# Composing the Fourier channel transform with the mixing weight, in a two-layer fp32 kernel with two more layers behind it

## The chip, the cores and the metric

One core of one Trainium2 chip. The metric is the device time of one execution in microseconds; a version's time is the median of its runs. The core's engines are TensorE (PE), ScalarE (ACT), VectorE (DVE), GpSimd (POOL) and SyncE (SP); SP and POOL issue the DMAs here.

## The reference

Four layers in sequence on 256 tokens of 2048 features; the change touches layers 0 and 1. There the input projection gives, among others, `u_f` of 1024 features in 8 groups of 128. What matters:

```
ug = u.reshape(B, S, 8, 128).astype(float32)
f  = real(fftn(ug, axes=(1, 3), norm="ortho"))   # over the tokens and over a group's channels
y  = einsum("bsgc,gcd->bsgd", f, w_fmix)         # a 128x128 matrix per group
y_f = y * silu(z_f)
```

The Fourier transform over the channels is a fixed 128x128 matrix (a cosine part and a sine part), and so is a map on the same index as `w_fmix[l][g]`. The rest of a layer is low-rank attention, gates, an output projection, a modulation from `c` (shift, scale, gate by the 2048 x 6144 matrix `w_ada[l]`) and two LayerNorms.

## The kernel before

**Plan and engines.** A Python class `Plan` (its method `whole`, L1096) writes one list of steps; then each engine's program (`sync` L1384, `gpsimd`, `tensor`, `scalar`, `vector`) walks that list and emits its own part of every step, in the list's order. So an engine's order is the plan's order, and an instruction that waits holds back what stands behind it on its engine.

**Weights.** Work comes as jobs, one per weight tile of two 128-row blocks (512 KB at most). `prep` (L163) issues the load into a slot on SP's queue (18 slots while the first stage lasts, 9 after it) and, for products in two halves, the split: ACT copies the tile to `whi` (the hi part, L1893 under the step `split`), DVE subtracts it to `wlo` (the lo part, L2214). PE then makes hi x hi, hi x lo and lo x hi products into the banks PM. `run` (L181) emits a job's products some jobs after its load and split; while the plan is `starting`, three jobs behind whatever their kind, later three weight tiles behind.

**Side work.** Everything small (rope, latent norms, Fourier groups, attention heads) is a generator with a `yield` per stage; `round` (L119) advances up to six of them once, twice per weight tile. Their products go to the banks PB: two while the first stage lasts, four later (`banks`).

**The Fourier groups**, `fourier(g)` in `mla` (L627), eight per layer, four started by `u_out` of each half of `u`:

1. `fs_mm` (L1736): two fp32 products with CSS, the transform over tokens, evicted by ACT (`fs`) to a `pbuf`.
2. `fc_mm` (L1743): two fp32 products with CF, cosine on columns 0 to 128 and sine on 129 to 255, evicted by ACT (`fc`) to a `ptbuf`.
3. `fw_mm` (L1750, product L1754): one fp32 product of 256 columns with `w_fmix[g]` in AR at FM; `fw` (L2019, L2431): ACT copies columns 0 to 128 to Z, DVE adds and subtracts the reflected sine part.

**The first stage.** `whole` interleaves the modulation of layer 0 (shift and scale; `ada_pe`, PE products of width 32 on raw tiles, `adap` and `adap_col`) with layer 0's first 24 weight tiles. There are eight k-pairs q; for each q three tiles j0, j1, j2 (one of three column groups each), with modulation tiles between them, and transposes (`trans`) of the normed input for the next q. Hooks `pre` and `after` hang steps on a job. After k-pair 5 the last rope table (`turn`) is made and `begin0` runs `mla_begin`, by which POOL loads `w_fmix` (L1454).

**Later.** Layer 0's gate part of the modulation and layer 1's modulation come as DVE multiply-adds (`ada`, L2127 on AC) between the other tiles. `ada_row` (POOL, L1464) stores a gate row and loads it, spread over the partitions, into GT; the output step of the layer reads GT on DVE (L2377). `w_out` ends a layer; in its fourth tile `late` adds `ln_load` (POOL, L1473), the two LayerNorm vectors of 1024 KB each. At the border `lead` (L1070) writes `post_norm` and `ln`, two normed quarters (`xn`), the sums of the scale's accumulators (`ada_col`, by `columns`), three transposes and the next layer's `begin` (so its `mla_begin`).

Of the kernel before, what the change touches and what calls it, by code (L numbers as in the profile page):

```python
# [61 lines left out]
class Plan:  # L62
# [364 lines left out]
    def post_norm(self, l):  # L427
# [28 lines left out]
        return self.step("post_norm", **s)  # L456

    def gate_post(self, l, blocks):
        def post(pair, mm):
# [69 lines left out]
    def w_out(self, l, w):  # L529
        for g in range(4):  # L530
            def late(g=g):
                if g == 0:
                    self.y_rest()
                    if l < 2:
                        self.ln_in = self.tick("ln_landed", 32)
                        self.step("ln_load", l=l, scores=("score_mm", self.count["score_mm"]))
                    if l == 2:
                        self.toep = self.tick("toep_landed", 96)
                        self.step("toep_windowed", logits=("sm_logit", self.count["sm_logit"]), pool=self.pool_mm)
            self.group([(w, g * 512, 512)], B2, self.out_post(l, g), late=late, early=l, final=g == 3)  # L540
# [3 lines left out]
    def mla(self, l):  # L544
# [3 lines left out]
        def begin():  # L548
            arf.extend(self.ar)
            Tk["fm"] = self.tick("fm_landed", 16)  # L550
            self.step("mla_begin", l=l, free=tuple(arf))

# [74 lines left out]
        def fourier(g):  # L627
# [10 lines left out]
            b, fr = yield from self.take(self.banks)  # L638
            mm = self.tick("fc_mm")
            self.step("fc_mm", bank=b, free=fr, buf=i, fs=a)  # L640
            self.pbuf.put(i, mm)
            yield
            i, ifree = yield from self.take(self.ptbuf)
            a = self.tick("fc")
            self.step("fc", bank=b, buf=i, bfree=ifree, mm=mm)
            self.banks.put(b, a)
            yield
            yield
            b, fr = yield from self.take(self.banks)
            mm = self.tick("fw_mm")  # L650
            self.step("fw_mm", g=g, bank=b, free=fr, buf=i, fc=a, fm=Tk["fm"])
            self.ptbuf.put(i, mm)
            yield
# [415 lines left out]

    def lead(self, first, trans, layer, columns=None):  # L1070

        n = len(self.jobs)
        begin = layer()

        def lead():
            first()
            self.normed((0, 1))
            if columns:
                columns()
            trans((0, 1, 2))  # L1080
            begin()

        def more(q):
            if q < 3:
                self.normed((q + 1,))
            trans((q + 2,))
            if q == 5:
                self.zw = self.h[KT - 1]
        self.jobs[n]["first"] = lead
        for q in range(8):  # L1090
            self.jobs[n + q]["fresh"] = True
        for q in range(1, 6):
            self.jobs[n + q]["pre"] = lambda q=q: more(q)
        return n

    def whole(self):  # L1096
# [27 lines left out]
        self.jobs.extend(ada[0][0])  # L1124

        def cols(q):
            ada[q][1]()
# [16 lines left out]
        for q in range(8):  # L1144
            j0, j1, j2 = (first[8 * g + q] for g in range(3))
            j0["last_chunk"] = q == 7
            self.jobs.append(j0)
            if q == 0:
# [44 lines left out]

        n1 = self.lead(norm1, lambda qs: self.mod_h(1, qs), lambda: self.mla(1), scale)
        self.w_out(1, "w_out1")
# [58 lines left out]
def build(nc, A):  # L1254
    with ExitStack() as ctx:
# [67 lines left out]
        def ar(o, n):  # L1323
            return AR[:, o:o + n]
# [92 lines left out]
        def gpsimd(e):  # L1417
# [30 lines left out]
            for kind, s in plan.order:  # L1448
                if kind == "biases":
# [3 lines left out]
                    e.dma_start(scr[32:64, :], AR[0:32, 2560:2944]).then_inc(SEM["scr_landed"], 16)  # L1453
                elif kind == "mla_begin":  # L1454
                    q.wait_all(s["free"])
                    e.dma_start(ar(FM, 1024).rearrange("p (g d) -> p g d", g=8),
# [43 lines left out]
        def tensor(e):  # L1500
# [7 lines left out]
            for kind, s in plan.order:  # L1508
# [227 lines left out]
                elif kind == "fs_mm":  # L1736
# [5 lines left out]
                    ins.then_inc(SEM["fs_mm"], 1)  # L1742
                elif kind == "fc_mm":  # L1743
                    q.wait_ge(s["fs"])
                    q.wait_all(s["free"])
                    T = pbuf(s["buf"])
                    for t, o in enumerate((slice(0, 129), slice(129, 256))):
                        ins = mm(B[:, o], CF[:, t, :], T[:, o], t == 0, True)
                    ins.then_inc(SEM["fc_mm"], 1)
                elif kind == "fw_mm":  # L1750
                    q.wait_ge(s["fc"])
                    q.wait_ge(s["fm"])
                    q.wait_all(s["free"])
                    e.matmul(B[:, 0:S], ar(FM + s["g"] * 128, 128), ptile(s["buf"])[:, 0:S], start=True, stop=True).then_inc(  # L1754
                        SEM["fw_mm"], 1)
                elif kind == "score_mm":
# [130 lines left out]
        def scalar(e):  # L1887
# [7 lines left out]
            for kind, s in plan.order:  # L1895
# [115 lines left out]
                elif kind == "fs":  # L2011
                    q.wait_ge(s["mm"])
                    q.wait_all(s["bfree"])
                    act(pbuf(s["buf"])[:, 0:S], B[:, 0:S]).then_inc(SEM["fs"], 1)
                elif kind == "fc":
                    q.wait_ge(s["mm"])
                    q.wait_all(s["bfree"])
                    act(ptile(s["buf"])[:, 0:S], B[:, 0:S]).then_inc(SEM["fc"], 1)
                elif kind == "fw":  # L2019
# [695 lines left out]
```

## Time and profile before

| what | value |
|---|---|
| median of 3 runs | 1558.52 us (1557.95 to 1561.76) |
| the profiled execution's own time | 1556.26 us |
| its span | 1554.4 us |
| granted TensorE clock, mean | 0.99 |
| PE busy | 1486.9 us, 96% |
| DVE, ACT, POOL busy | 1065.7, 706.8, 45.3 us |
| DMA | 347.15 MB, mean 223 GB/s |

The span is the time between the first and the last instruction of the profiled execution; the execution's own time has 1.86 us more around it. PE's ends are modelled, so that PE busy is not PE at its peak. An fp32 product is written as two records. The chain of work that ended last is followed back from the last instruction, at each step to what released it; "issue" is time in which the engine waited for nothing that the profile shows.

### The profile page before, as it was taken

The page shows a single profiled execution, that of the slowest core. Times are in us where ns is not written, and L with a number is a line of the kernel's source. Part 1 is how long each engine was busy: PE and PEld are TensorE (multiplying, and loading weights), DVE is VectorE, ACT ScalarE, POOL GpSimd, SP SyncE. Part 2 cuts the span into 40 slices and gives each one's busy share as a digit, 9 for nine tenths or more (in the row PEclk, how much of TensorE's full clock was granted, in tenths as well). Part 3 has the DMA queues.
Part 4 walks back from the last instruction along what each step waited for, and adds up shares of the span by engine and source line. Part 5 has one row for each costly group of instructions (what it writes and reads, how often), then busy time and mean ns, then how long its engine had stood idle before and what let it go on. Part 6 is the DMA issues. An engine that isn't in the chain of part 4 may idle for free.

```text
span 1554.4 us, 25460 instructions
## 1 busy us (share of the span) xinstructions
PE 1486.9 (96%) x10123; PEld 1316.1 (85%) x10123; DVE 1065.7 (69%) x1732; ACT 706.8 (45%) x1218; POOL 45.3 (3%) x66
## 2 busy tenths in 40 slices
PE   5999999989979999999979999999998999999999
PEld 3778789988869788998859997799987998889987
DVE  3348689899987667577575684875655667775653
ACT  2235234344345445444335444654444546665442
POOL 3000000000000000000000000010000000000000
PEclk9999999999989999999999999999999999999999
DMA  9999889998837556776745555466665554445673
GB/s 357 406 406 330 283 294 364 348 365 338 329 90 266 191 195 207 251 247 205 217 148 179 177 169 151 123 219 187 184 196 163 151 162 121 124 123 160 183 223 98
DMA packets 102126, 347.15 MB, mean 223 GB/s; under 512 B 11392, under 2 KB 21876, under 8 KB 101240
## 3 DMA queue, kind: packets, MB, share of 16 engines
q1 hardware_dynamic: 96888, 327.42, 62.7%
q0 software_dynamic: 5120, 18.11, 3.5%
q8 instruction: 80, 1.31, 0.3%
q14 instruction: 38, 0.31, 0.1%
HBM read 343.27 MB, written 2.21 MB: 222 GB/s over the span
## 4 chain that ended last, share of the span: by engine, by line
PE 78%; DVE 11%; issue 4%; DMA 4%; ACT 3%; SPq 0%; DVEq 0%; ACTq 0%
PE PM L1506 66%; PE PB L1506 8%; DVE wlo L2214 2%; DMA stg<-in_w_in 2%; DVE AC L2127 2%; ACT whi L1893 1%; DVE X L2127 1%; DMA stg<-in_w_ada 1%; ACT AR L1893 1%; PE PB L1741 1%; PE PB L1713 1%; PE PB L1816 1%; DVE SM L2127 0%; PE PB L1788 0%; ACT Hh L1893 0%
## 5 line engine op out<-in xcount | busy, mean ns | idle before, releaser
L2214 DVE TENSOR_TENSOR wlo<-stg,whi 128x1024 fp32r<-128x1024 f32 (+2 forms) x417 | 497.9, 1203 | 324.5 <-ACT whi L1893 322.2
L1893 ACT ACTIVATE whi<-stg 128x1024 fp32r<-128x1024 f32 (+2 forms) x417 | 430.3, 1038 | 455.2 <-PE PM L1506 348.5
L1506 PE MATMUL PM<-Hh,whi 128*128 128x256 f32 x1824 | 526.2, 291 | 11.5 <-DVE wlo L2214 7.6
L1506 PE MATMUL PM<-Hh,wlo 128*128 128x256 f32 x1776 | 500.3, 285 | 0.0
L1506 PE MATMUL PM<-Hl,whi 128*128 128x256 f32 x1824 | 497.7, 284 | 0.0
L1506 PEld LDWEIGHTS PM<-Hh,whi 128*128 128x128 f32 x1824 | 352.4, 193 | 29.5 <-issue 17.0
L1506 PEld LDWEIGHTS PM<-Hh,wlo 128*128 128x128 f32 x1776 | 343.6, 193 | 0.0
L1506 PEld LDWEIGHTS PM<-Hl,whi 128*128 128x128 f32 x1824 | 342.5, 193 | 0.4
L1506 PE MATMUL PM<-whi,Hh 128*128 128x512 f32 (+1 forms) x576 | 223.3, 389 | 0.4 <-DVE wlo L2214 0.4
L1506 PE MATMUL PM<-wlo,Hh 128*128 128x512 f32 (+1 forms) x576 | 220.1, 383 | 0.0
L1506 PE MATMUL PM<-whi,Hl 128*128 128x512 f32 (+1 forms) x576 | 218.3, 384 | 0.0
L2127 DVE SCALAR_TENSOR_TENSOR AC<-stg,CA,AC 128x1024 f32<-128x1024 f32 x120 | 153.6, 1280 | 6.6 <-DMA stg<-in_w_ada 4.0
L1506 PEld LDWEIGHTS PM<-whi,Hh 128*128 128x128 f32 x576 | 108.3, 188 | 23.4 <-issue 1.5
L1506 PEld LDWEIGHTS PM<-wlo,Hh 128*128 128x128 f32 x576 | 108.3, 188 | 21.0 <-issue 0.2
L1506 PEld LDWEIGHTS PM<-whi,Hl 128*128 128x128 f32 x576 | 107.1, 188 | 21.4
L1506 PE MATMUL PM<-whi,ARL 128*128 128x512 f32 (+1 forms) x272 | 86.1, 383 | 0.0
L1893 ACT ACTIVATE AR<-PB 128x384 f32<-128x384 f32 (+2 forms) x110 | 47.3, 471 | 75.4 <-PE PB L1506 28.0
L1506 PE MATMUL PB<-AR 64*128 64x256 f32 (+4 forms) x576 | 71.1, 353 | 3.5 <-ACT AR L1893 2.2
L1506 PEld LDWEIGHTS PB<-AR 64*128 64x128 f32 (+2 forms) x576 | 46.2, 170 | 21.2 <-issue 6.0
L1506 PEld LDWEIGHTS PM<-whi,ARL 128*128 128x128 f32 x272 | 51.1, 188 | 10.3 <-issue 0.4
L1506 PE MATMUL PM<-wlo,ARL 128*128 128x512 f32 (+1 forms) x144 | 54.4, 378 | 0.0
L1893 ACT ACTIVATE AR<-PM 128x256 f32<-128x256 f32 (+2 forms) x58 | 24.1, 466 | 57.1 <-PE PM L1506 57.1
(287 smaller groups left out, 1389.5 us busy)
## 6 DMA issues: line engine op xcount, KB each, us to landing
stg<-in_w_ada SPq DMA_DIRECT2D x163, 512.0 KB, 6.2
stg<-in_w_in SPq DMA_DIRECT2D x105, 512.0 KB, 5.4
stg<-in_even_w_in SPq DMA_DIRECT2D x80, 512.0 KB, 3.6
stg<-in_odd_w_in SPq DMA_DIRECT2D x72, 512.0 KB, 3.6
stg<-in_w_out SPq DMA_DIRECT2D x64, 512.0 KB, 4.5
stg<-in_even_w_out SPq DMA_DIRECT2D x32, 512.0 KB, 3.6
stg<-in_odd_w_out SPq DMA_DIRECT2D x32, 512.0 KB, 3.5
AR<-in_w_ada SPq DMA_DIRECT2D x29, 512.0 KB, 14.5
```

The lines of the kernel that those rows point to most:

```text
L1506: return e.matmul(out, l, r, start=start, stop=stop, skip_group_check=True)
L1713: ins = e.transpose(B[:, kk * S + t * 128:kk * S + t * 128 + 128], XN[:, t, k * 128:(k + 1) * 128], IDN[:, :])
L1741: ins = e.matmul(B[:, 0:S], ar(UU + t * 1024 + s["g"] * 128, 128), CSS[:, t, :], start=t == 0, stop=t == 1)
L1816: ins = e.transpose(B[:, n * 128:(n + 1) * 128], L[:, n * 128:(n + 1) * 128], IDN[:, :])
L1893: return e.activation(out, x, f, **k)
L2127: return e.scalar_tensor_tensor(out=out, in0=in0, scalar=scalar, in1=in1, op0=op0, op1=op1)
L2214: e.tensor_tensor(wlo[s["slot"]][:, :, 0:n], stg[s["slot"]][:, :, 0:n], whi[s["hi"]][:, :, 0:n].bitcast(F32), ALU.subtract).then_inc(SEM[" ...
```

## The change

Each layer composes the two matrices once: CF's cosine and sine part (stationary) times four groups of `w_fmix` (512 columns), four products in all per layer, evicted by ACT to GT as [cosine part, 8 groups | sine part, 8 groups]. The symmetric CF makes the product the wanted left factor. A group's `fc_mm`, `fc` and `fw_mm` become one `fw_mm` of two products with the composed blocks, straight from the `pbuf`. Layer 0's four are hung on j0 of k-pairs 4 to 7 (`after`), layer 1's stand in `lead` behind the norm. `w_fmix` of layer 0 is loaded at the end of POOL's constants, that of layer 1 in `late` of layer 0's `w_out`, ahead of `ln_load`. The gate rows of a layer, which go to the same GT, wait for the layer's eighth `fw_mm`.

```
--- before.py
+++ after.py
@@ -455,6 +455,14 @@
         self.h_free = self.mm_last
         return self.step("post_norm", **s)
 
+    def compose(self, l, i):
+        b, fr = self.now(self.banks)
+        mm, u = self.tick("comp_mm"), self.tick("comp")
+        self.step("comp", l=l, i=i, bank=b, free=fr, mm=mm, gt_free=[t for t in self.gate_free if t] if i == 0 else ())
+        self.banks.put(b, u)
+        if i == 3:
+            self.comp_mm = mm
+
     def gate_post(self, l, blocks):
         def post(pair, mm):
             if blocks[-1] == KT - 1:
@@ -531,6 +539,9 @@
             def late(g=g):
                 if g == 0:
                     self.y_rest()
+                    if l == 0:
+                        self.tick("fm_landed", 16)
+                        self.step("fm_load", l=1, used=self.comp_mm)
                     if l < 2:
                         self.ln_in = self.tick("ln_landed", 32)
                         self.step("ln_load", l=l, scores=("score_mm", self.count["score_mm"]))
@@ -547,8 +558,8 @@
 
         def begin():
             arf.extend(self.ar)
-            Tk["fm"] = self.tick("fm_landed", 16)
-            self.step("mla_begin", l=l, free=tuple(arf))
+            Tk["comp"] = ("comp", 4 * l + 4)
+            self.gate_free = [("fw_mm", 8 * l + 8)] * 4
 
         def raw_post(first, n):
             def post(pair, mm):
@@ -636,20 +647,9 @@
             yield
             yield
             b, fr = yield from self.take(self.banks)
-            mm = self.tick("fc_mm")
-            self.step("fc_mm", bank=b, free=fr, buf=i, fs=a)
+            mm = self.tick("fw_mm")
+            self.step("fw_mm", g=g, bank=b, free=fr, buf=i, fs=a, comp=Tk["comp"])
             self.pbuf.put(i, mm)
-            yield
-            i, ifree = yield from self.take(self.ptbuf)
-            a = self.tick("fc")
-            self.step("fc", bank=b, buf=i, bfree=ifree, mm=mm)
-            self.banks.put(b, a)
-            yield
-            yield
-            b, fr = yield from self.take(self.banks)
-            mm = self.tick("fw_mm")
-            self.step("fw_mm", g=g, bank=b, free=fr, buf=i, fc=a, fm=Tk["fm"])
-            self.ptbuf.put(i, mm)
             yield
             a, c = self.tick("fw"), self.tick("fw_z")
             self.step("fw", g=g, bank=b, mm=mm, zw=self.zw, fw=a)
@@ -1067,13 +1067,15 @@
         out += extra[e:]
         self.jobs.extend(out)
 
-    def lead(self, first, trans, layer, columns=None):
+    def lead(self, first, trans, layer, columns=None, compose=None):
 
         n = len(self.jobs)
         begin = layer()
 
         def lead():
             first()
+            if compose:
+                compose()
             self.normed((0, 1))
             if columns:
                 columns()
@@ -1123,6 +1125,9 @@
                   lambda: turn(0), lambda: turn(1)]
         self.jobs.extend(ada[0][0])
 
+        self.step("fm_load", l=0, used=None)
+        self.tick("fm_landed", 16)
+
         def cols(q):
             ada[q][1]()
 
@@ -1144,6 +1149,8 @@
         for q in range(8):
             j0, j1, j2 = (first[8 * g + q] for g in range(3))
             j0["last_chunk"] = q == 7
+            if q > 3:
+                j0["after"] = lambda i=q - 4: self.compose(0, i)
             self.jobs.append(j0)
             if q == 0:
                 pair(1, 0)
@@ -1191,7 +1198,11 @@
             for fin in self.scale_sums:
                 fin()
 
-        n1 = self.lead(norm1, lambda qs: self.mod_h(1, qs), lambda: self.mla(1), scale)
+        def compose():
+            for i in range(4):
+                self.compose(1, i)
+
+        n1 = self.lead(norm1, lambda qs: self.mod_h(1, qs), lambda: self.mla(1), scale, compose)
         self.w_out(1, "w_out1")
         ex = []
         for c0 in (2 * D, 2 * D + 1024):
@@ -1451,8 +1462,8 @@
                     e.dma_start(scr[0:32, :], AR[0:32, 896:1280]).then_inc(SEM["scr_landed"], 16)
                     q.wait_ge(("buckets", 2))
                     e.dma_start(scr[32:64, :], AR[0:32, 2560:2944]).then_inc(SEM["scr_landed"], 16)
-                elif kind == "mla_begin":
-                    q.wait_all(s["free"])
+                elif kind == "fm_load":
+                    q.wait_ge(s["used"])
                     e.dma_start(ar(FM, 1024).rearrange("p (g d) -> p g d", g=8),
                                 A["w_fmix"][s["l"]].rearrange("g c d -> c g d")).then_inc(SEM["fm_landed"], 16)
                 elif kind == "ada_bias":
@@ -1740,19 +1751,20 @@
                     for t in range(2):
                         ins = e.matmul(B[:, 0:S], ar(UU + t * 1024 + s["g"] * 128, 128), CSS[:, t, :], start=t == 0, stop=t == 1)
                     ins.then_inc(SEM["fs_mm"], 1)
-                elif kind == "fc_mm":
+                elif kind == "fw_mm":
                     q.wait_ge(s["fs"])
-                    q.wait_all(s["free"])
-                    T = pbuf(s["buf"])
+                    q.wait_ge(s["comp"])
+                    q.wait_all(s["free"])
+                    T, g = pbuf(s["buf"]), s["g"] * 128
                     for t, o in enumerate((slice(0, 129), slice(129, 256))):
-                        ins = mm(B[:, o], CF[:, t, :], T[:, o], t == 0, True)
-                    ins.then_inc(SEM["fc_mm"], 1)
-                elif kind == "fw_mm":
-                    q.wait_ge(s["fc"])
-                    q.wait_ge(s["fm"])
-                    q.wait_all(s["free"])
-                    e.matmul(B[:, 0:S], ar(FM + s["g"] * 128, 128), ptile(s["buf"])[:, 0:S], start=True, stop=True).then_inc(
-                        SEM["fw_mm"], 1)
+                        ins = mm(B[:, o], GT[:, t * 1024 + g:t * 1024 + g + 128], T[:, o], t == 0, True)
+                    ins.then_inc(SEM["fw_mm"], 1)
+                elif kind == "comp":
+                    t, j = s["i"] // 2, s["i"] % 2
+                    q.wait_all(s["free"])
+                    q.wait_ge(later)
+                    q.wait_ge(("fm_landed", 16 * s["l"] + 16))
+                    e.matmul(B[:, :], CF[:, t, :], ar(FM + 512 * j, 512), start=True, stop=True).then_inc(SEM["comp_mm"], 1)
                 elif kind == "score_mm":
                     h = s["h"]
                     q.wait_ge(s["q"])
@@ -2012,10 +2024,10 @@
                     q.wait_ge(s["mm"])
                     q.wait_all(s["bfree"])
                     act(pbuf(s["buf"])[:, 0:S], B[:, 0:S]).then_inc(SEM["fs"], 1)
-                elif kind == "fc":
-                    q.wait_ge(s["mm"])
-                    q.wait_all(s["bfree"])
-                    act(ptile(s["buf"])[:, 0:S], B[:, 0:S]).then_inc(SEM["fc"], 1)
+                elif kind == "comp":
+                    q.wait_ge(s["mm"])
+                    q.wait_all(s["gt_free"])
+                    act(GT[:, 512 * s["i"]:512 * s["i"] + 512], B[:, :]).then_inc(SEM["comp"], 1)
                 elif kind == "fw":
                     q.wait_ge(s["mm"])
                     q.wait_ge(s["zw"])
```

## Rows read from the trace of the kernel before

**Rows 1.** the page: busy time (us, share, instructions) and the chain that ended last
```profile
PE 1486.9 (96%) x10123; PEld 1316.1 (85%) x10123; DVE 1065.7 (69%) x1732; ACT 706.8 (45%) x1218; POOL 45.3 (3%) x66
...
PE 78%; DVE 11%; issue 4%; DMA 4%; ACT 3%; SPq 0%; DVEq 0%; ACTq 0%
```

**Rows 2.** busy time by stage; the first line names the columns
```profile
core 0: us, PE busy (x) PEld busy (x) DVE busy (x) ACT busy (x) POOL busy (x), PEclk, DMA share, GB/s
...
80.00:93.00 13.00, 13.00 (x124) 10.05 (x128) 5.63 (x11) 2.91 (x4) 1.02 (x2) 1.00 1.03 406
...
140.00:217.00 77.00, 74.61 (x367) 62.62 (x368) 58.50 (x98) 20.28 (x49) 3.52 (x3) 1.00 0.83 295
...
251.00:330.00 79.00, 74.92 (x607) 73.55 (x604) 70.74 (x76) 32.27 (x47) 1.05 (x2) 1.00 0.94 358
...
520.00:592.00 72.00, 69.05 (x415) 60.08 (x414) 43.55 (x67) 30.60 (x59) 3.58 (x2) 1.00 0.60 202
...
446.00:451.00 5.00, 0.15 (x1) 0.07 (x1) 4.80 (x24) 0.66 (x1) 0.56 (x1) 0.50 0.42 105
```

**Rows 3.** pieces of the chain (start, us) and a rope product of layer 1
```profile
157.85 1.02 PE PB L1754 x4
...
161.64 0.86 PE PB L1754 x4
...
189.30 0.45 PE PB L1754 x2
...
569.08 0.67 PE L1720 MATMUL PB<-AR,ROT 128*128 128x256 f32 x2 [0.19 <-ACT AR L1893]
```

**Rows 4.** timeline (start, us): fp32 products of 512 columns and evictions of 128x512
```profile
438.64 3.70 PE L1506 MATMUL PM<-X,TMP 128*128 128x512 f32 x8 [1.14 <-DVE TMP L2345]
439.87 0.60 ACT L1893 ACTIVATE X<-PM 128x512 f32<-128x512 f32 x1 [11.19 <-PE PM L1506]
...
140.92 1.07 ACT L1893 ACTIVATE AR<-PB 128x512 f32<-128x512 f32 x2
```

**Rows 5.** the load stage: timeline of ACT and DVE, then pieces of the chain
```profile
93.15 0.85 ACT L1893 ACTIVATE whi<-stg 128x768 fp32r<-128x768 f32 x1 [1.39 <-DMA stg<-in_w_in]
...
98.48 0.38 ACT L1893 ACTIVATE AC<-PB 128x256 f32<-128x256 f32 x1 [4.49 <-PE PB L1506]
...
94.03 0.96 DVE L2214 TENSOR_TENSOR wlo<-stg,whi 128x768 fp32r<-128x768 f32 x1 [0.61 <-ACT whi L1893]
...
96.55 1.86 PE PB L1506 x32
98.41 2.35 PE PM L1506 x18
```

**Rows 6.** pieces of the chain at the load stage's end
```profile
136.38 1.05 ACT whi L1893
...
138.60 0.43 DVE AR L2389
```

**Rows 7.** POOL's timeline, and a piece of the chain
```profile
191.27 0.56 POOL L1471 DMA_DIRECT2D GT<-g_scratch  x1 [3.40 <-DMA g_scratch<-TMP]
...
251.84 0.53 POOL L1477 DMA_DIRECT2D AR<-in_ln_g  x1 [8.93 <-PE PB L1506]
...
445.65 0.92 POOL L1456 DMA_DIRECT2D AR<-in_w_fmix  x1 [192.76 <-DVE X L2127]
...
251.71 9.32 DMA stg<-in_w_in
```

**Rows 8.** timeline of the border between the layers
```profile
442.18 3.97 PE L1506 MATMUL PB<-ONE,AC 128*128 128x1 f32 x32
...
443.43 2.00 ACT L1893 ACTIVATE Z<-X,SM 128x2048 f32<-128x2048 f32 x1
...
450.34 1.52 ACT L1893 ACTIVATE Z<-X,SM 128x512 f32<-128x512 f32 x2 [4.81 <-DVE SM L2127]
...
451.03 2.79 PE L1713 MATMUL PB<-IDN,Z 128*128 128x128 f32 x12 [4.88 <-DVE Z L2333]
```

## The prediction

> **What bounds the kernel now.** I read the page first. PE is busy for 1486.9 of 1554.4 us and 78% of the chain that ended last is PE, with 11% on DVE [rows 1]. An edit of PE work counts where the chain lies on PE, and the chain's lines say in which stages that is so. So the next view is the table by stage [rows 2]. Up to 134.5 us, while the modulation weights come in, PE has 13.00 busy of 13 us and at the same time DMA moves 406 GB/s, the highest rate of the table: both are full. From 140 to 217 us (layer 0's second Fourier half, queries) PE has 74.61 of 77 us, DMA share 0.83. From 251 to 330 us the chain is no longer PE's: DMA share 0.94 at 358 GB/s, DVE 70.74 of 79 us. From 520 to 592 us (layer 1's Fourier groups and queries) PE has 69.05 of 72 us and DMA only 202 GB/s. At the border between the layers, 446 to 451 us, PE has 0.15 of 5 us.
>
> **What the change removes.** Per group it drops one fp32 product of 256 columns (L1754), one ACT eviction of 128x256 and a semaphore round between; per layer eight of each. The profile writes each such product as two records. The chain prices it: x4 (two groups) takes 0.86 us, so 0.43 us a product and 3.44 us a layer. In layer 0 the chain holds 1.02 + 0.86 + 0.45 us of them and once more 0.86, in all 3.2 us [rows 3]; I take **-3.2 us**. Bounds: -3.8 with a little for each change between fp32 and fp32r products saved, 0 if the DMA and DVE bound stage from 217 us on starts no earlier. I stay near the full value, because the chain runs on PE up to there without a step through a DMA. In layer 1 the stage is PE's alone. Four pairs make 3.44; a rope product there also sat idle 0.19 us behind ACT's eviction of the old chain [rows 3]. I take **-3.7 us**, bounds -3.4 and -5 (three fewer planner rounds per group, and DVE's reflected adds come earlier in its queue). The evictions themselves lie beside PE work and are worth nothing unless something waits for them.
>
> **What it adds: four products of 512 columns per layer, each with a 128x512 eviction into GT.** The nearest row is the border's own fp32 product of that shape: x8 records, four products, in 3.70 us [rows 4]. So 0.9 us each, 3.7 a layer: PE's columns are the same before and after, only the place moves. ACT's eviction of the first begins 1.23 us after the product began (438.64, 439.87), and two such evictions take 1.07 us, so the next ACT instruction comes 0.54 us later [rows 4].
>
> **Layer 0's four**, behind the first weight tile of k-pairs 4 to 7, the first near 96.5 us, the last near 134.5. This stage has no idle PE [rows 2], so the 0.9 us counts. There is more: ACT works in its written order, and the hi part of the *next* weight tile is written behind the new eviction. Today that hi copy (0.85 us at 93.15) runs while PE is still in the tile before it; the DVE lo part follows 0.88 us later, and PE comes to that tile at 98.41, after 1.86 us of modulation products [rows 5]. After the change: product at 96.5, eviction 1.23 us later, 0.54 to the copy, 0.88 to the lo part, 1.0 to PE: 3.65 us. PE has 0.9 + 1.86 = 2.76 us to do meanwhile, so it stands for 0.9 us. The same order is at work today: the eviction at 98.48 sat 4.49 us for PE [rows 5], and the next hi copy stood behind it. k-pairs 4 and 5 cost 1.8 us each. k-pair 6: 1.6, since the next modulation columns wait for a lo part on DVE already today and so eat a little of it. k-pair 7: its eviction pushes the hi copy at 136.38, so the lo part and the raw copy at 138.60 [rows 6], behind which stands the rope product near 140 us; 0.9 + 0.5 = 1.4. Sum **+6.6 us**. Bounds: 3.0 (the products alone, a little absorbed) and 8.0.
>
> The Trainium skill, TensorE: Matmul & The Clock Gate, Architectural detail, says that ScalarE and VectorE are strict FIFO. The trace agrees in the wait of 4.49 us [rows 5]; if ACT could reorder, the stalls would fall away and this stage would cost 3.7 us.
>
> **The w_fmix loads.** Layer 0's 512 KB go from behind the rope tables in POOL's queue to the end of the constants, near 25 us, both in a full DMA stage: I take 0, since the order of the same bytes changes and PE is as full; bound +1.5, the load's own time, if a weight tile lands later for it. Layer 1's go from 445.65, where DMA has little to do, to ahead of the two LayerNorm rows at 251.84 [rows 7]. That is where the chain holds a weight load of 9.32 us. 524288 B at the 358 GB/s of that stage [rows 2] are 1.46 us; bounds 0 and 1.5, I take **+1.2 us**, because this load already shares the queues with the LayerNorm rows. On POOL nothing but the 0.9 us of issue lies before the LayerNorm rows, which are wanted at 438. POOL's new wait for gate rows on the eighth Fourier product: in layer 0 that product takes the place of the cosine products around 185 us, and the row is loaded at 191.27 [rows 7], so 0. If it came 6 us later, it would hold back only a bias add some 30 us behind.
>
> **Layer 1's four**, at the border. PE ends the norm's products at 442.2 and goes to the column sums of the scale; the four new ones come between and fill it to 445.8. ACT is in its square until 445.4, then evicts four at 0.54, done near 447.7, before its next work at 450.34 [rows 8]. The column sums of the scale (3.97 us) [rows 8] need the first evicted bank, so run 446.1 to 450.1; transposes wait for DVE till 451.03. Cover: 0.9 us on PE, 2.6 on ACT; if the sums were 1 us longer, transposes would slip. 0 for the work. The granted clock was 0.50 from 446 to 451 [rows 2], so 1.2 GHz, and PE came out of an idle of 4.88 us into twelve records of transposes that took 2.79 us [rows 8]. With idle down to 0.9 us a part of that may come back: **-0.3 us** (bounds -1.4, half the transposes' time, and +1.0).
>
> **Sum:** 6.6 + 1.2 - 3.2 - 3.7 - 0.3 = +0.6 us. The profiled execution took 1556.26 us (span 1554.4 and 1.86 around it) and would become 1556.9. The median of the three runs, 1558.52, lies 2.26 above it; on it the forecast is 1559.1. A measurement of this kernel can tell 0.3%, 4.7 us, from no change: faster is below 1553.8, slower above 1563.2.
>
> **Rivals.** *The load stage gives cover* (0.16). DMA is full at 406 GB/s until 120 us and loads are queued ahead; if the stage's end is set by the last bytes, PE's 6.6 us vanish and the rest stands: -6.0, 1552.5. For it: the hi copy at 93.15 had itself waited 1.39 us for a landing [rows 5]. Against: PE has no idle time, and SP is waiting for slots that PE frees.
> *Slower, by the ACT queue of the load stage* (0.13): each eviction of a composed block holds the hi copy that PE needs next, 7.6 us in sum, while layer 0's 3.2 us are lost at 217 us, where DVE and DMA take over. 7.6 + 1.5 - 0 - 3.7 = +5.4, 1563.9. It decides once the stall behind each eviction exceeds 0.9 us and nothing of the saving passes 217 us.
> *The clock at the border* (0.10): the new products keep PE at 2.4 GHz into the transposes. At twice the clock their 2.79 us would be 1.4 [rows 8]; if all of it is on the path that is 1.1 more than the 0.3 I took: 1558.0. The Trainium skill, TensorE: Matmul & The Clock Gate, What's actually happening, says that the gate follows PE's recent activity; the trace agrees (0.50 in the idle stretch), and by that rule the time is this one.
> *Forecast* (0.61): load stage pays, the two Fourier stages repay.
>
> **How the numbers follow.** Forecast and clock case lie within 0.3%: 0.71 same. Faster 0.16, slower 0.13. All terms at their low ends come to -7.2 (1551.3), all at their high ends to +8.6 (1567.1); 1552.2 to 1564.0 leaves out about half of each outer rival.
>
> **What would show it.** Four 128x512 evictions into GT between 97 and 136 us, each followed at once by a hi copy, and PE idle by 0.9 us on "DVE wlo" behind three of them; the first Fourier products of layer 0 (L1741) some 6.6 us later. At 217 us a lag of about 3.4. At the border no PE wait on ACT. At 592 us a lag of 0 to 1. It is wrong if the lag at 140 us is below 3 or above 8, if the lag grows between 140 and 251 us, or if layer 1's Fourier stage does not shorten by over 3 us.

## The result, and the profile after

The changed kernel is slower. Its median is **1566.46 us** (1564.25 to 1568.17, five runs) against 1559.72 us (1557.95 to 1561.76, five runs) of the kernel before on the same chip: a ratio of 1.0040, with a 95% interval of 1.0026 to 1.0054. The profiled execution took 1568.17 us, its span 1566.3 us. The forecast was 1559.1, with a range of 1552.2 to 1564.0. The result lies above the range, and the most likely case, no change, did not happen.

The page after, busy time and the chain that ended last, against [rows 1]:

```profile
PE 1492.2 (95%) x10107; PEld 1316.3 (84%) x10107; DVE 1067.9 (68%) x1732; ACT 705.3 (45%) x1210; POOL 45.3 (3%) x66
...
PE 79%; DVE 9%; DMA 5%; ACT 4%; issue 3%; SPq 0%; DVEq 0%; ACTq 0%
```

PE issues 16 records fewer but is busy 5.3 us longer, and the DMA share of the chain goes from 4% to 5%. The stages, with the columns of [rows 2]:

```profile
92.00:140.00 48.00, 45.67 (x398) 33.95 (x397) 26.16 (x47) 21.21 (x30) 0.00 (x0) 1.00 0.93 355
140.00:217.00 77.00, 73.77 (x358) 61.98 (x357) 58.03 (x94) 20.08 (x46) 3.52 (x3) 0.96 0.83 287
...
251.00:330.00 79.00, 75.40 (x593) 72.51 (x592) 66.54 (x74) 28.37 (x43) 1.06 (x2) 1.00 0.93 352
...
520.00:592.00 72.00, 69.03 (x372) 59.32 (x371) 48.27 (x70) 31.22 (x54) 2.95 (x1) 0.98 0.57 195
```

From 92 to 140 us, where DMA moved 390 GB/s before, it moves 355. Some 11 GB/s of that is the 512 KB of `w_fmix` itself, issued at 123.50 us before and at 25.50 now. The rest fits PE freeing the slots later, so that loads start later; no run isolates that. The chain of the load stage after, against [rows 5] (start, us, what):

```profile
95.83 3.06 PE PM L1517 x24
98.89 0.88 PE PB L1767 x2
99.76 0.02 issue
99.78 0.02 ACT GT L1905
99.81 0.07 issue
99.88 0.02 ACTq L1255
99.89 0.39 issue
100.28 0.84 ACT whi L1905
101.12 0.02 issue
101.14 0.97 DVE wlo L2226
102.11 0.04 issue
102.16 0.86 PE PM L1517 x5
```

L1767 is the new product. Before, the chain ran 3.05, 1.86, 2.35 on PE alone. Now it leaves PE behind the product and goes through the eviction into GT, the hi copy, the lo part and back: 3.27 us from the product's start to the next weight tile, where 1.86 us of PE work used to be. So the first product costs 1.41 us, of which 0.88 is the product and 0.53 a stall of PE. ACT in the same place (timeline: start, duration):

```profile
99.78 0.60 ACT L1905 ACTIVATE GT<-PB 128x512 f32<-128x512 f32 x1 [5.69 <-PE PB L1767]
100.28 0.83 ACT L1905 ACTIVATE whi<-stg 128x768 fp32r<-128x768 f32 x1
```

ACT stood for 5.69 us in front of the eviction, with the hi copy behind it in its queue. Before, that copy was done at 94.0 [rows 5], over four microseconds before PE wanted it.

The border after: the four products and ACT's four evictions.

```profile
455.72 3.60 PE L1767 MATMUL PB<-AR,CF 128*128 128x512 f32 x8
459.60 3.73 PE L1517 MATMUL PB<-ONE,AC 128*128 128x1 f32 x32 [0.29 <-ACT GT L1905]
```

PE waits 0.29 us for the bank of the column sums, and nothing else there waits for ACT. The transposes behind the column sums, and busy time and clock over them, after and then before (columns as in [rows 2]):

```profile
464.57 2.79 PE L1724 MATMUL PB<-IDN,Z 128*128 128x128 f32 x12 [1.24 <-DVE Z L2345]
```

```profile
464.50:467.50 3.00, 2.93 (x14) 2.94 (x15) 1.55 (x7) 2.70 (x6) 0.00 (x0) 0.50 0.00 0
```

```profile
451.00:454.00 3.00, 2.97 (x14) 2.98 (x15) 1.56 (x7) 2.70 (x6) 0.00 (x0) 0.50 0.00 0
```

PE's idle time before them went from 4.88 to 1.24 us, and they take 2.79 us at a granted clock of 0.50 all the same.

**Lags.** To see where time goes I take the n-th hi copy (ACT, "whi") of each trace, the same work in every kernel, and subtract its start in the first trace of before. The next table has one profiled execution per column, microseconds, the rows named by the time in the trace of before. *Control* is the unchanged kernel profiled a second time and *again* the changed one. The other names are those of the experiments: *all late* is the kernel with all three repairs, *fm0 alone* and *fm1 alone* are the kernel before with one of the two loads early.

| at | control | after | again | fm1 late | j2 | evict late | all late | layer 1 | fm0 alone | fm1 alone |
|---|---|---|---|---|---|---|---|---|---|---|
| 31.3 | -0.3 | 2.0 | 1.6 | 2.2 | 2.2 | 1.7 | 0.4 | -0.1 | 1.9 | -0.1 |
| 85.2 | -2.0 | 2.3 | 0.4 | 2.1 | 2.4 | 1.6 | 0.5 | -0.9 | 2.2 | -1.8 |
| 136.4 | -1.0 | 7.2 | 5.3 | 7.0 | 3.6 | 4.2 | 1.4 | -0.8 | 2.2 | -1.0 |
| 150.5 | 2.3 | 10.6 | 8.7 | 7.0 | 4.6 | 4.2 | 5.7 | 0.9 | 3.9 | 0.7 |
| 231.7 | 2.5 | 7.1 | 6.3 | 5.6 | 1.3 | 2.1 | 4.0 | 1.6 | 4.1 | 2.4 |
| 345.8 | 3.2 | 13.5 | 13.0 | 9.5 | 5.2 | 5.0 | 4.2 | 2.3 | 7.5 | 5.5 |
| 475.8 | 3.2 | 13.5 | 13.0 | 9.5 | 5.2 | 5.1 | 4.3 | 2.2 | 7.5 | 5.4 |
| 569.6 | 3.2 | 11.9 | 9.7 | 7.8 | 1.9 | 1.8 | 2.6 | 0.6 | 9.1 | 7.0 |
| 1540.4 | 3.1 | 11.9 | 9.8 | 7.9 | 2.0 | 1.9 | 2.6 | 0.4 | 9.2 | 6.6 |

The control is 3.1 us late at the end with no change at all, which comes between 136.4 and 150.5 us, where its clock is lower (below). So a single profile places a cost, and only the medians weigh it.

### The profile page after: what moved, and what is told of

It is laid out like the page before. It is cut to its first block, busy times and chain, and to the rows that moved or that the text cites. A ratio compares the mean times of both kernels' runs of the same rounds, so it can differ in the third digit from the quotient of the medians.

```text
span 1566.3 us, 25412 instructions
## 1 busy us (share of the span) xinstructions
PE 1492.2 (95%) x10107; PEld 1316.3 (84%) x10107; DVE 1067.9 (68%) x1732; ACT 705.3 (45%) x1210; POOL 45.3 (3%) x66
## 4 chain that ended last, share of the span: by engine, by line
PE 79%; DVE 9%; DMA 5%; ACT 4%; issue 3%; SPq 0%; DVEq 0%; ACTq 0%
PE PM L1517 67%; PE PB L1517 7%; DMA stg<-in_w_in 4%; DVE wlo L2226 2%; ACT whi L1905 1%; DMA stg<-in_w_ada 1%; DVE AC L2139 1%; PE PB L1752 1%; DVE X L2139 1%; ACT AR L1905 1%; PE PB L1828 1%; PE PB L1724 1%; DVE SM L2139 0%; PE PB L1800 0%; DVE AR L2590 0%
## 5 line engine op out<-in xcount | busy, mean ns | idle before, releaser
L1905 ACT ACTIVATE AR<-PB 128x384 f32<-128x384 f32 (+2 forms) x94 | 41.6, 486 | 67.5 <-PE PB L1517 28.8
```

Source lines behind the costliest of these rows:

```text
L1905: return e.activation(out, x, f, **k)
```

## The experiments

All were timed in rounds together with the kernel before. The ratios, with 95% intervals:

| kernel | median us (n) | ratio to before |
|---|---|---|
| the change again | 1565.32 (6) | 1.0036 [1.0024, 1.0048] |
| layer 1's load late | 1561.04 (12) | 1.0008 [1.0000, 1.0017] |
| layer 0's load late | 1561.56 (12) | 1.0014 [1.0003, 1.0025] |
| layer 0's products and evictions on j2 | 1559.16 (12) | 1.0005 [0.9990, 1.0020] |
| evictions alone later | 1560.30 (11) | 1.0003 [0.9993, 1.0014] |
| both loads late | 1559.75 (11) | 0.9999 [0.9990, 1.0008] |
| both loads late, products on j2 | 1557.43 (12) | 0.9980 [0.9968, 0.9992] |
| layer 0 alone, in that form | 1560.70 (12) | 1.0001 [0.9991, 1.0011] |
| layer 1 alone, its load late | 1556.65 (7) | 0.9975 [0.9960, 0.9991] |
| before, layer 0's load early | 1563.01 (12) | 1.0016 [1.0006, 1.0026] |
| before, layer 1's load early | 1562.59 (12) | 1.0016 [1.0008, 1.0025] |
| before, as it is | 1559.79 (11) | 0.9996 [0.9987, 1.0004] |

The kernel before had 1560.03, 1560.02 and 1559.84 us in the three groups of runs. 0.001 in a ratio is 1.6 us.

**The change again.** No edit.

> The changed kernel once more, unedited, for a second profile. Theory A (three fixed costs): the lag against the kernel before is again 7 us at the end of the load stage (hi copy of the tile near 136 us), grows by 4 to 6 us between 247 and 273 us, where the w_fmix load of layer 1 stands ahead of the LayerNorm rows, and falls by 3 us in layer 1's Fourier stage; ratio 1.004. Theory B (chance of the clock): the half-clock stretch at 150 us and the growth at 250 us are not there again, the lag at 330 us is 5 or less and the profiled execution is nearer 1562.

It was slower by 0.0036, so the result repeats: +5.6 us by this ratio, +6.2 by the first. From 85.2 to 136.4 us the lag grows by 4.9 us again and in layer 1's Fourier stage it falls by 3.3, as theory A had it. The growth at the gate comes otherwise: from 244.9 to 272.2 us it is 1.7 us and not 4 to 6, and most of the rest comes later, up to 333 us. The stretch of lower clock at 150 us is there again, its sixteen products in 6.00 us.

**Layer 1's w_fmix load behind the LayerNorm rows.**

```
 def late(g=g):
+    if g == 2 and l == 0:
+        self.tick("fm_landed", 16)
+        self.step("fm_load", l=1, used=self.mm_last)
     if g == 0:
         self.y_rest()
-        if l == 0:
-            self.tick("fm_landed", 16)
-            self.step("fm_load", l=1, used=self.comp_mm)
...
```

> The change with one edit: layer 1's w_fmix load is issued two column groups later in layer 0's output projection, behind the LayerNorm rows. Theory A (the load collides in the stage bound by DMA): 4 to 5 us less than the change, ratio to the kernel before 1.001; the weight loads near 260 us land within 9 us of their issue. Theory B (only its bytes count, 1.5 us): ratio 1.003. Theory C (the load is not in the way; the lag there comes from the load stage): ratio 1.004, no difference.

It takes 0.0028 from the change (1.0036 to 1.0008), 4.4 us. That is more than the 1.2 us of my forecast and more than the load's bytes. The sign of theory A did not come: the chain's DMA piece at the gate still lasts 13.31 us.

**Layer 0's w_fmix load behind the table of gains**, and no longer ahead of the weights:

```
+        def gains():
+            table("gains", "vec")
+            self.step("fm_load", l=0, used=("adap_out", 3))
+            self.tick("fm_landed", 16)
...
-        self.step("fm_load", l=0, used=None)
-        self.tick("fm_landed", 16)
```

> The change with one edit: layer 0's w_fmix load waits until the third set of modulation columns is evicted (about 57 us in) instead of being issued near 25 us. Theory A (the early load delays the weight tile that PE needs at 41 us in the changed kernel): the lag at the tile of 58 us goes from 2.3 to 0, the kernel gets 2 us faster, ratio 1.003. Theory B (that lag is the chance of the early clock): no difference, ratio 1.004.

It takes 0.0022 from the change, 3.4 us, and the lag at 31.3 us falls from 2.0 (after) to 0.1. I had forecast 0 for this load.

**Layer 0's products and evictions on j2**, the third job of the k-pair, in place of j0:

```
-            if q > 3:
-                j0["after"] = lambda i=q - 4: self.compose(0, i)
...
+            def behind(q=q):
+                if q < 6:
+                    tables[q - 1]()
+                if q > 3:
+                    self.compose(0, q - 4)
+            j2["after"] = behind
```

> The change with one edit: layer 0's four composing products hang on the third weight tile of k-pairs 4 to 7 instead of the first, so that their evictions stand ahead of no hi copy that PE needs next. Theory A (0.9 us of product and 0.9 us of stall behind each): the stalls go, the products stay, the lag at the end of the load stage is 3.6 to 4.2 instead of 7.2 us, 3 us faster, ratio 1.002. Theory B (PE's time alone counts and the stall is absorbed): lag at 140 us unchanged, ratio 1.004. Theory C (the stage has cover from DMA): lag near 0.

The same products on the same engines. At 136.4 us the lag has grown by only 1.2 us, but the hi copy of that row stands behind three of the four evictions here and behind all four in the change. With the fourth, at 150.5 us, it has grown by 2.1 (2.43 to 4.57, no clock dip in this trace), where the change has 4.9: the order costs 2.8 us in the load stage. The ratio falls by 0.0031, 4.8 us. This alone does not say whether PE's place or ACT's place is what counts.

**The eviction alone moved.** The product stays on j0; only ACT's eviction goes behind the second job (j1) of the k-pair:

```
-        self.step("comp", l=l, i=i, bank=b, free=fr, mm=mm, gt_free=[t for t in self.gate_free if t] if i == 0 else ())
-        self.banks.put(b, u)
+        self.step("comp", l=l, i=i, bank=b, free=fr)
+
+        def evict():
+            self.step("comp_ev", i=i, bank=b, mm=mm, gt_free=[t for t in self.gate_free if t] if i == 0 else ())
+            self.banks.put(b, u)
+
+        if l == 0:
+            self.ev_later = evict
+        else:
+            evict()
...
+            def behind(q=q):
+                if q > 3:
+                    self.ev_later()
+                if q < 7:
+                    cols(q + 1)
+            j1["after"] = behind
             if q < 7:
-                j1["after"] = lambda q=q: cols(q + 1)
...
```

> The change with one thing undone: layer 0's four products stay where they are on PE, but the eviction of each is put into ACT's queue after the next third of its k-pair (j1) and not right behind the product. If the order of ACT's queue is what costs (the w_in copy waits for the eviction, and that for the product), the load stage falls from +4.9 us to +1 to +2 at 136 us and the time to 1560 to 1561, as when product and eviction were both moved. If the products' place on PE is what costs, it stays at +4.9 and 1565.

1560.30 against the change's 1565.32. Only ACT's order differs, so ACT's order is what costs these 5 us. The load stage shows 2.3 of them (from 85.2 to 150.5 us the lag grows by 2.6 in place of 4.9); the rest does not show there, and the gate stage, where these single traces grow by 2.9 and by 6.4 to 6.8 us, is where they part further. I have not shown by what route. ACT in this kernel, timeline:

```profile
94.61 0.85 ACT L1918 ACTIVATE whi<-stg 128x768 fp32r<-128x768 f32 x1 [1.25 <-DMA stg<-in_w_in]
...
101.23 1.05 ACT L1918 ACTIVATE whi<-AR 128x1024 fp32r<-128x1024 f32 x1
102.17 0.59 ACT L1918 ACTIVATE GT<-PB 128x512 f32<-128x512 f32 x1
```

The hi copy runs at 94.6 as it did before, ahead of the product, and the eviction comes where nothing is wanted at once. The chain there:

```profile
98.15 0.86 PE PB L1780 x2
99.01 1.86 PE PB L1530 x32
100.88 2.35 PE PM L1530 x18
```

PE goes from the product straight into its 1.86 and 2.35 us. The lag grows by 2.6 us from 85.2 to 150.5 us, four products of 0.86 less 0.9 that slack takes up.

**Both loads late, products and evictions as in the change**, which leaves their order alone as the difference to the next one:

> The change with both w_fmix loads late and the products where the change has them. Against e4_all (1557.4) it has the order of the products alone: if their order costs its 3.7 us (4.9 less 1.2 in the load stage) whatever else is repaired, 1561, ratio 1.0007. If the two loads were what made the order dear, 1558, ratio 0.9985.

It fell between the two expectations. Against the next kernel it is 0.0019 slower, 3.0 us, and the two intervals overlap by 0.0002 only. The 3.7 us of the expectation compared unlike rows of the table, as said above; rightly read, the order costs 2.8 us in the load stage of the traces, and 3.0 here. With both loads early the same step gave 4.8; the intervals are too wide to say whether the loads make the order dearer.

**All three repairs:**

> The change with all three repairs together: layer 1's w_fmix load behind the LayerNorm rows, layer 0's behind the table gains, and layer 0's four products hung behind the third job of each k-pair and not the first. If the three costs add (2 us for the early load, 3.6 us for the order of the products, 3 us for layer 1's load), it ends 8 us under the change: 1557, ratio 0.998 to the kernel before. If the gate stage returns whatever was won before it, only the border and layer 1 keep their gain less what the products still cost: 1559 to 1560, ratio 0.9995 to 1.000.

1557.43, ratio 0.9980: this kernel beats both. It lies 8 to 9 us under the change, as the first expectation had it. Taken out of the change one at a time, the three costs gave 4.4, 3.4 and 4.8 us, 12.6 together, where all at once give 8.7: they may overlap, though each difference is known to some 2 us only.

**Layer 1 alone composed, its load late**; layer 0 in two steps as before:

```
...
-            Tk["comp"] = ("comp", 4 * l + 4)
+            if l == 0:
+                Tk["fm"] = self.tick("fm_landed", 16)
+                self.step("mla_begin", l=l, free=tuple(arf))
+                return
+            Tk["comp"] = ("comp", 4)
...
-            if q > 3:
-                j0["after"] = lambda i=q - 4: self.compose(0, i)
```

> Layer 1 alone is composed, at the border, with its w_fmix load behind the LayerNorm rows of layer 0's gate; layer 0 computes its Fourier part in two steps as before. If the border carries the four products at no cost and layer 1's saving reaches the end whole: -3.5 us, 1556.5, ratio 0.9978. If the products cost the border their 3.5 us: 1560, ratio 1.000.

1556.65, ratio 0.9975: the full gain of layer 1 reaches the end. It is the fastest of all, though its interval overlaps that of the kernel with all three repairs.

**Layer 0 alone composed, in the repaired form:**

> Layer 0 alone is composed, in the form with its load behind the table gains and its products behind the third job of each k-pair; layer 1 computes its Fourier part in two steps as before. From e4_all less e6_layer1_only: the four products cost the load stage about what the Fourier stage saves, 1560.8, ratio 1.0005. If layer 0's saving of 3.4 us reached the end it would be 1557.5, ratio 0.9985.

1560.70, ratio 1.0001: even in its best form here, layer 0's part is worth nothing that can be measured. That is a balance of two parts. Its four products in this form cost the load stage 2.1 us (the lag of *j2*), so about 1.9 us of the saving in the Fourier stage must have reached the end (0.4 to 3.5 by the interval).

**The kernel before with layer 0's load moved to the start,** nothing composed:

```
-            Tk["fm"] = self.tick("fm_landed", 16)
-            self.step("mla_begin", l=l, free=tuple(arf))
+            Tk["fm"] = ("fm_landed", 16 * l + 16)
+            if l:
+                self.tick("fm_landed", 16)
+                self.step("mla_begin", l=l, free=tuple(arf))
...
         self.jobs.extend(ada[0][0])
+        self.step("mla_begin", l=0, free=())
+        self.tick("fm_landed", 16)
```

> The kernel before with layer 0's w_fmix load alone moved to the very start, nothing composed. Theory A (the load takes the DMA engines its bytes while PE stands still for the first weights, and nothing gives that back before 140 us): the first w_in copies come 1.4 to 2 us later, and so does the end: 1561.5, ratio 1.001. Theory B (the later stages, that also wait for DMA, hand it back, because the same load is then not made at 140 us): 1560, ratio 1.000. With no fixed cost in the load stage, e2b_fm0_late's 3.8 us under the change would be more than this load can explain, and part of it would belong to the change's other costs meeting it.

+2.5 us by the ratio, against nothing in my forecast. The pieces of the chain at the start, first of this kernel and then of the unchanged one's second profile, show where:

```profile
21.14 19.52 DMA stg<-in_w_in
40.69 1.06 ACT whi L1897
```

```profile
20.99 17.75 DMA stg<-in_w_in
38.77 1.07 ACT whi L1893
```

The w_in tile of this piece lands 1.92 us later, and PE waits for it in both. (In the first trace of before the chain stays on PE there.)

**The kernel before with layer 1's load moved ahead of the LayerNorm rows,** nothing composed:

```
+                    if l == 0:
+                        self.tick("fm_landed", 16)
+                        self.step("mla_begin", l=1, free=(("fw_mm", 8),))
...
-            Tk["fm"] = self.tick("fm_landed", 16)
-            self.step("mla_begin", l=l, free=tuple(arf))
+            Tk["fm"] = ("fm_landed", 16 * l + 16)
+            if l == 0:
+                self.tick("fm_landed", 16)
+                self.step("mla_begin", l=l, free=tuple(arf))
```

> The kernel before with one part of the change alone: layer 1's w_fmix load is issued ahead of the LayerNorm rows in layer 0's gate and no longer at layer 1's start. Nothing is composed. Theory A (a load of 512 KB in a stage that the DMA engines bound costs its bytes, 524288 B at 352 GB/s): +1.5 us, 1561.5. Theory B (this load is what returns the saving of layer 0's Fourier stage in the gate stage): +3 to +4 us, 1563.5, ratio 1.002. Theory C (the saving before 217 us is given back in that stage whatever is loaded there): 0, 1560, ratio 1.000.

+2.5 us by the ratio (1.3 to 3.9), between theories A and B. The chain's piece "DMA stg<-in_w_in" at the gate, 9.32 us before [rows 7]:

```profile
252.66 13.16 DMA stg<-in_w_in
265.84 1.07 ACT whi L1898
```

That length does not belong to this load alone. In the kernel before with layer 0's load early, where layer 1's comes at the border as ever, the piece is

```profile
255.59 12.10 DMA stg<-in_w_in
```

With neither load early it lasts 10.41 us (both loads late) and 10.52 us (all three repairs).

**The unchanged kernel again:**

> The kernel before once more, as it is, for a second profiled execution of it. It tells how far single executions of one kernel lie apart at each landmark of the trace. If the half-clock stretches lie where each execution happens to put them, this one shows some of them in other places than the first profile and its landmarks differ by up to 3.4 us from it with no change at all; if they belong to the kernel's own stream of work, the landmarks agree within 1 us. Time 1560, ratio 1.000.

The time is the same (0.9996), and the landmarks of the table move by up to 3.2 us. Its stage from 137 to 150 us, against the changed kernel's 150 to 157 us, columns as in [rows 2]:

```profile
137.00:150.00 13.00, 11.58 (x50) 10.05 (x49) 10.19 (x23) 4.92 (x10) 0.00 (x0) 0.74 0.73 251
```

```profile
150.00:157.00 7.00, 7.00 (x21) 5.74 (x21) 5.43 (x18) 2.10 (x4) 0.00 (x0) 0.51 0.67 218
```

In both the granted clock falls towards the lower level, 1.2 GHz, as PE comes out of the waits at the end of the load stage; in the first trace of before it comes out of the same waits at 1.00. The first sixteen Fourier products of layer 0 lie there. As a piece of the chain they take 3.56 us in the first trace of before, 5.23 in the control, and this in the changed kernel and in the one with layer 1's load late:

```profile
150.91 6.61 PE PB L1752 x16
```

```profile
150.41 3.56 PE PB L1752 x16
```

So of the 11.9 us by which the two first profiles differ at the end, some 3 us are no part of the change.

## Why the prediction was wrong

**The load stage, +6.6.** The mechanism was right: four products, each followed by an eviction with the hi copy behind it, and PE idle on the lo part. Its size was too large by 1.7 us. From 85.2 to 136.4 us the lag grew by 4.9 us (2.33 to 7.21), and the hi copy of that last row stands behind the fourth eviction, so this is the price of all four: 1.5, 1.5, 1.1 and 0.8 us (the chain's pieces at 104.32, 117.57, 127.49 and 138.60 us of before come at 108.13, 122.84, 133.90 and 145.81). I had 1.8, 1.8, 1.6 and 1.4. The stall of the first was 0.53 us and not 0.9: I let the eviction start 1.23 us after its product began, read from a merged row of four products, and it started after 0.89 (98.89, 99.78).

**Layer 0's load, 0, is the step that failed first.** I argued that "the order of the same bytes changes and PE is as full". PE is not full there. Busy time from 20 to 60 us in the first trace of before, and then in the control:

```profile
20.00:60.00 40.00, 33.05 (x273) 24.39 (x265) 9.73 (x17) 10.15 (x16) 3.17 (x6) 0.91 1.03 405
```

```profile
20.00:60.00 40.00, 31.74 (x289) 23.81 (x286) 11.21 (x22) 10.26 (x16) 3.17 (x6) 0.83 1.03 404
```

DMA has no gap in that stretch and PE has seven to eight microseconds of them. In the control and in every kernel with the load early the chain hangs there on a w_in tile for 18 to 20 us, so what is put ahead of that tile is waited for. Alone the load costs 2.5 us (0.9 to 4.1), more than my bound of 1.5 though the interval reaches below it; taking it out of the change gives 3.4. I had read the busy share of the slice from 80 to 93 us for a load issued near 25 us.

The Trainium skill, Perfetto Trace Analysis, Engine Utilization, says that when only one core of a pair is active it may pull more than the 358 GB/s of its share of the memory, but is bounded by its 16 DMA engines at about 435 GB/s. The trace agrees, with the 404 and 405 GB/s of the rows above, above the share and below the bound.

**Layer 1's load, +1.2.** Mis-sized: alone it costs 2.5 us (1.3 to 3.9). I took the bytes' time. The chain's DMA piece at the gate is 3.8 us longer in that trace (9.32 to 13.16 us), but as layer 0's load alone makes it 2.8 us longer too, it does not show how the 2.5 us come about.

**Layer 0's saving, -3.2.** It is there: the pieces of [rows 3] are gone and the lag falls between 150.5 and 231.7 us by 3.4 (after) and 2.4 (again), where it rises by 0.2 to 1.8 in the kernels that leave layer 0 as it was. How much of it passes 217 us is not settled. Layer 0 alone, repaired, ends at +0.2 us (-1.4 to +1.7) though its products cost 2.1 in the load stage, so some 1.9 us arrive there; with both loads late 1.2 arrive (4.9 - 3.9 - 1.2 = -0.2, the measured difference). In the change the medians leave no room for any. I had named this as the bound of the term and taken the other end, "because the chain runs on PE up to there". That looks at the way into the stage and not at what its end hangs on.

**Layer 1's saving and the border, -3.7 and -0.3.** The saving was right: the ratio of layer 1 alone gives -3.9 us (-6.2 to -1.4), and the traces without a clock dip in that stage (again, j2, evict late) show the lag fall by 3.3 each from 475.8 to 569.6 us. The four products at the border cost nothing, as forecast: DVE's norm is what the chain hangs on there, and PE still stands idle 1.24 us behind it. The wait of 0.29 us on ACT was to be absent. The -0.3 us for the clock did not come: the transposes take 2.79 us as before, at a granted clock of 0.50.

**The sum.** With the sizes as measured one by one and nothing for layer 0's saving, 4.9 + 2.5 + 2.5 - 3.9 = +6.0 us, where the forecast had +0.6 and the runs give +5.6 to +6.2. With the 2.4 to 3.4 us by which the lag falls in layer 0's Fourier stage it would be +2.6 to +3.6. So either this saving is lost in the change, or the costs together are 2 to 3 us dearer than one by one; each price is known to some 1.5 us, and the runs do not tell the two apart. From the other end, taking the repaired kernel (-3.1) and adding the order (3.0) and the two loads (2.5 each) gives +4.9, which agrees with the change within the intervals.

**What stays open** is the rest in the gate stage. From 231.7 to 345.8 us the lag grows by 6.4 and 6.8 us in the two profiles of the change, by 3.0 and 3.6 where only layer 1's load is early (alone; in the change with layer 0's late), by 3.4 and 3.9 where only layer 0's is (alone; in the change with layer 1's late), which adds no byte there, by 0.2, 0.7, 1.0 and 2.3 in the kernels with neither early, and by 0.7 in the control. With both early and the products or evictions moved it grows by 3.9 and 2.9 only. An early load of layer 0 thus seems to return a second time in that stage. These are single executions, and I have not shown by what route.

**The rivals.** "Slower, by the ACT queue of the load stage" gave 1563.9 and was nearest, with 0.13. That was in part luck. Of its two conditions the stall of over 0.9 us did not hold (0.53), and whether nothing of the saving passes 217 us is open. It had 7.6 us for the load stage, where 4.9 came, and 1.5 for the loads, where 2.5 each came. "The load stage gives cover" was wrong: PE's lag ran through. "The clock at the border" was wrong too: the clock over the transposes was 0.50 with PE's idle time before them cut from 4.88 to 1.24 us, and with none left in the trace of *j2*. Of my checks, that the lag must not grow between 140 and 251 us was met with growth in the first profile (7.2 us at 136.4, 10.4 at 251.3), all of it after 231.7, where the waits of the gate begin; in the repeat it went from 5.3 to 5.9.

## What to carry to other kernels

An eviction put into a strict queue ahead of a prefetch copy delays the copy until its product is done: hang it behind the copies that are due next, and here the same work cost some 3 us less for four of them. A load moved into a full DMA stage is paid for where someone waits for the load behind it; look for the longest DMA piece of the chain downstream of its issue, and price it by that tile, not by the busy share of some other slice. Look at where the added work will stand. Layer 0's four products stood in a stage that PE fills and cost 2.1 us at best, about what the saving brought to the end; layer 1's stood at a border where PE waits for DVE and cost nothing, and the same edit gave its whole 3.9 us. So try such a change one layer at a time.

## What the runs showed of the hardware

The granted clock of TensorE dips at different places in executions of one and the same kernel: the control had it at 0.74 from 137 to 150 us, where the first trace of before had 1.00. The same sixteen products took 3.56 us without it and 5.23 to 6.61 us with it, so a comparison of two profiles of this kernel by stages is uncertain by some 3 us though both have a mean clock of 0.98 to 0.99. What places a dip I could not tell from these traces.

At the border the clock over the twelve transpose records was 0.50, and they took 2.79 us, with 4.88 us of idle time of PE before them (before), with 1.24 (after) and with none (*j2*).
